# Order of the matmuls and of the activation steps in the up pass of a decoder layer

## The chip, the cores and the metric

One core of one Trainium2 chip runs one layer of a hybrid decoder. The metric is the device time of one execution in microseconds (us). The kernel before takes 1964.89 us, the median of three runs (1959.94 to 1966.12).

## What is computed

Two request groups (512 prompt tokens and 8 x 4 decode tokens, 544 in all) go through a mixer (attention and pooling) and then a feed-forward part; only the second one is touched here:

```python
def ffn_sublayer(x, w_up, w_down, g_pre, g_post):
    h = rmsnorm(x, g_pre)
    a = jnp.square(jax.nn.relu(jnp.einsum('ntd,df->ntf', h, w_up)))
    return x + rmsnorm(jnp.einsum('ntf,fd->ntd', a, w_down), g_post)
```

`w_up` is 2048 x 8192, `w_down` 8192 x 2048, all in float32.

## The kernel before

**Precision.** Every product is made of three matmuls in the rounded format fp32r: an operand is split into a high part (its rounded value) and a low part (what is left), and high x high, high x low and low x high are summed in one PSUM bank.

**The up pass.** The 8192 columns of `w_up` are taken in 32 blocks of 256. The first two are computed plainly; the other 30 (`UP_GROUPS`) are "groups" `G` of Strassen's method: seven products (`NP = 7`) of half-size matrices in place of eight. Product `N` is `G, i = divmod(N, NP)`, with `i` from 0 to 6. One product is 8 pairs of tiles, and so 24 matmuls of 128 x 128 weights by 272 columns. In `strassen_product` (line 2238) they are issued as 8 couples, high weight by high activation (L2263) and the same weight by low activation (L2264), then 8 with the low weight (L2268). Group G of the up pass is product 7G to 7G+6. The down pass follows, with products of 12 matmuls each.

**Who does what, for each product N.** ScalarE (ACT) rounds the weight twice: `high_copy` (L1169) into PSUM and `high_part` (L1178) into SBUF. VectorE (DVE) subtracts in `low_part` (L1669). GpSimd (POOL) makes four weight combinations in each group: t1 (L871), t3 (L876), t2 (L885), t4 (L891); i = 2 of a group needs t2, i = 3 t1, i = 4 t3 and i = 6 t4. DVE takes each product out of its bank and adds it into a quadrant sum: `take` (L1693, a copy, or L1696, an addition). A bank can only be written again after its `take`: by `taken_before` (line 2232) i = 2 of group G waits for the take of i = 0, and i = 5 for that of i = 3.

**The activation steps, once in a group.** When the takes of group G are done, DVE applies `relu` (L1703, after the take of the next group's i = 0), ACT squares (`square_mlp`, L1193), POOL forms four sums of quadrants (L899 to L904, `activation_sums`), ACT rounds seven rows (`mlp_high`, L1199), and DVE subtracts in two steps (`mlp_low`, L1715: three rows, then four). SyncE (SP) stores the result to HBM: high rows (L655), then the low rows (L660).

**What sets the order.** Each engine runs its instructions in program order; the loops are written out by hand. ACT's loop is `for N in range(4, N_ALL)` (line 1246), with `square_mlp(G + 1)` behind i = 3 and `mlp_high(G + 1)` behind i = 4. DVE's loop (line 1787) is, for each N: `take(N)`, `relu` where i = 0, `low_part(N + 3)`, and then `mlp_low(G + 1, 0)` where i = 3 and `mlp_low(G + 1, 1)` where i = 4. POOL's loop (line 911) is t4, activation sums, t1, t3, t2 of the next group. SP's queue, lines 689 to 694, is

```python
for g in range(1, UP_GROUPS - 1):
    store_hi(g + 1)
    store_lo(g + 1)
    if g < UP_GROUPS - 2:
        blocks_split(g)
        load_up(g + 2)
```

`store_lo` waits for each of the two steps of `mlp_low`; `load_up` fetches the 2 MB of weights of a group in four transfers (L626). t1 and i = 0 of a group wait for all four.

Of the kernel before, what the change touches and what calls it, by code (L numbers as in the profile page):

```python
# [24 lines left out]
def hybrid_decoder(nc, x_prompt, x_sample, cache_k, cache_v, state_pool, w_in, w_out, w_pool, pool_scale,  # L25
# [50 lines left out]
    UP_GROUPS = F_GROUPS - PLAIN  # L76
# [20 lines left out]
    with ExitStack() as ctx:  # L97
# [369 lines left out]
        STARTS = (True, True, False, True, False, False, False)  # L467
# [35 lines left out]
        def split_of(N, which):  # L503
            if N < N_UP:
                return splits[:, (N + 1) % 2 if N < NP else (N + 2) % 3, which, :].rearrange("p (j c) -> p j c", c=P)
            d = N - N_UP
            return splits[:, (2, 0)[d % 4 // 2], which, d % 2 * 512:(d % 2 + 1) * 512].rearrange("p (j c) -> p j c", c=P)
# [45 lines left out]
        for c, (bank, col) in enumerate(SPREAD_AT):  # L553
            first = c * P
            while first < c * P + tok_rows[c]:
# [4 lines left out]
                first = last  # L560
# [374 lines left out]
        def _(act):  # L935
# [160 lines left out]
            def square(src, count, par, tmp=sq_tmp):  # L1096


                group = 0 if not isinstance(count, int) else count // KT
                if isinstance(count, int) and count % KT < 2:  # L1100
                    if group:
                        act.wait_ge(sums_turned, group)
                else:
                    act.wait_ge(sq_added, count - 1 - group)
                nc.scalar.activation(tmp[:, par * T:(par + 1) * T].rearrange("p (h t) -> p h t", h=2), src,
                                     ACT.Square).then_inc(sq_ready, 1)
# [53 lines left out]
            def high_copy(N):  # L1160

                source_ready(N)
                if N < HIGH_FROM:
                    return
                if N < HIGH_FROM + 2:
                    act.wait_ge(relued, 4)
                if high_free(N):
                    act.wait_ge(part_lo, high_free(N))
                nc.scalar.activation(high_of(N).bitcast(F32R), weight_of(N), ACT.Copy).then_inc(hi_copied, 1)  # L1169

            def high_part(N):
                if N < 2:
                    act.wait_ge(unit_used, U_END - 1 + N)
                if N == NP + 2:
                    act.wait_ge(squared, PLAIN)
                if split_free(N):
                    act.wait_ge(product_done, split_free(N))
                nc.scalar.activation(split_of(N, 0), weight_of(N), ACT.Copy).then_inc(part_hi, 1)  # L1178
# [9 lines left out]
            def square_mlp(f):  # L1188
                act.wait_ge(relued, 4 * (f + 1) if f < PLAIN else 4 * PLAIN + 2 * (f - PLAIN + 1))
                if f == 1:  # L1190
                    act.wait_ge(lo_stored[0], 16)
                src = plain_rows if f == 1 else mlp_rows
                nc.scalar.activation(mlp_rows[:, 0:4, :], src[:, 0:4, :], ACT.Square).then_inc(squared, 1)  # L1193

            def mlp_high(g):
                act.wait_ge(a_summed, 4 * g + 4)
                if g > 0:
                    act.wait_ge(hi_stored, 16 * g)
                nc.scalar.activation(mlp_hi[:], mlp_sums[:], ACT.Copy).then_inc(mlp_rounded, 1)  # L1199
# [46 lines left out]
            for N in range(4, N_ALL):  # L1246
                high_copy(N)
                high_part(N)
                G, i = divmod(N, NP)
                if N == 5:  # L1250
                    mlp_high(1)
                if i == 3 and 0 < G < UP_GROUPS:
                    square_mlp(G + 1)
                if i == 4 and 0 < G < UP_GROUPS:
                    mlp_high(G + 1)
                if N == N_UP + NP + 3:
                    square_mlp(F_GROUPS - 1)
                if N == N_UP + 2 * NP + 2:
                    mlp_high(F_GROUPS - 1)
                n = G - (ALL_G - OUT_PAIRS)  # L1260
                if i == 5 and n > 0:
                    for nt in range(2):
                        m = 2 * (n - 1) + nt
                        act.wait_ge(taken, NP * G)
                        square(y_sum[:, m, :].rearrange("p (h t) -> p h t", h=2), 2 * KT + m, nt, sqf_tmp)
# [19 lines left out]
        def _(dve):  # L1285
# [385 lines left out]
            def take(N):  # L1671

                G, i = divmod(N, NP)
                dve.wait_ge(product_done, N + 1)
                src = banks[:, bank_of(G, i), 0:H]
                if G < UP_GROUPS:
                    at_quad = QUAD_AT[GOES_TO[i]]
                    dst, fresh = quads[:, at_quad + (G % 2 if at_quad == 3 else 0), :], FRESH[i]
                    if i == 0:
                        dve.wait_ge(h_summed, 4)  # L1680
                    if i == 0 and G > 1:
                        dve.wait_ge(relued, 4 * PLAIN + 2 * (G - 1))
                    if i == 2 and G > 0:
                        dve.wait_ge(relued, 4 * PLAIN + 2 * G)
                else:
                    c, n = divmod(G - UP_GROUPS, OUT_PAIRS)
                    dst, fresh = y_quad(n, GOES_TO[i]), FRESH[i] and c == 0
                    if c == 0 and n == 4 and i == 0:
                        dve.wait_ge(hi_stored, 16 * F_GROUPS)
                        for one in lo_stored:  # L1690
                            dve.wait_ge(one, 16 * F_GROUPS)
                if fresh:
                    nc.vector.tensor_copy(dst, src).then_inc(taken, 1)  # L1693
                else:
                    dve.wait_ge(taken, N)
                    nc.vector.tensor_tensor(dst, dst, src, ALU.add).then_inc(taken, 1)  # L1696
# [90 lines left out]
            for N in range(NP, N_UP):  # L1787
                take(N)
                G, i = divmod(N, NP)
                if i == 0:  # L1790
                    relu(G - 1)
                if N < N_UP - 3:
                    low_part(N + 3)
                elif N == N_UP - 3:
                    low_part(N_UP)
                    low_part(N_UP + 1)
                if i == 3:
                    mlp_low(G + 1, 0)
                if i == 4:
                    mlp_low(G + 1, 1)  # L1800
            low_part(N_UP + 2)
            low_part(N_UP + 3)
# [5 lines left out]
            for N in range(N_UP, N_ALL):  # L1808
# [8 lines left out]
                G, i = divmod(N, NP)  # L1817
# [32 lines left out]
        def _(pe):  # L1850
# [381 lines left out]
            def taken_before(G, i):  # L2232


                last_group = NP * (G - 1)
                return (last_group, last_group + 2, NP * G + 1, last_group + 6, NP * G + 3, NP * G + 4, NP * G + 5)[i]

            def strassen_product(N):
                G, i = divmod(N, NP)
                if N in (0, 1, 3, NP):  # L2240
                    pe.wait_ge(relued, {0: 5, 1: 6, 3: 7, NP: 8}[N])
                pe.wait_ge(part_hi, N + 1)
                if taken_before(G, i) > 0:
                    pe.wait_ge(taken, taken_before(G, i))
                if G == 0:
                    pe.wait_ge(hp_lo, H_READY[i])
                if G >= UP_GROUPS and (G - UP_GROUPS) % OUT_PAIRS == 0:
                    c = (G - UP_GROUPS) // OUT_PAIRS
                    pe.wait_ge(mlp_landed[i], 16 * (c + 1))
                out = banks[:, bank_of(G, i), 0:H]  # L2250
                pairs = UP_J if G < UP_GROUPS else DOWN_J

                def parts(j):
                    if G < UP_GROUPS:
                        return h_part(i, 0)[:, j, :], h_part(i, 1)[:, j, :]
                    c = (G - UP_GROUPS) // OUT_PAIRS
                    return mlp_parts[c % 2][i][:, j, 0, :], mlp_parts[c % 2][i][:, j, 1, :]

                for j in range(pairs):
                    xh, xl = parts(j)  # L2260
                    wh = split_of(N, 0)[:, j, :]
                    first = STARTS[i] and j == 0
                    nc.tensor.matmul(out, wh, xh, start=first, stop=False, skip_group_check=not STARTS[i])  # L2263
                    nc.tensor.matmul(out, wh, xl, start=False, stop=False, skip_group_check=not STARTS[i])  # L2264
                pe.wait_ge(part_lo, N + 1)
                for j in range(pairs):
                    xh, _ = parts(j)
                    ins = nc.tensor.matmul(out, split_of(N, 1)[:, j, :], xh, start=False, stop=j == pairs - 1,  # L2268
                                           skip_group_check=not STARTS[i])
                ins.then_inc(product_done, 1)  # L2270
# [69 lines left out]
```

## Time and profile before

| | |
|---|---|
| median of three runs | 1964.89 us |
| the profiled execution | 1960.73 us |
| its span, first to last instruction | 1959.0 us |
| TensorE (PE) busy | 1919.4 us, 98% |
| DVE, ACT, POOL busy | 67%, 64%, 44% |
| DMA engines, 1 queue of SP | 48.7% |
| granted TensorE clock, mean | 0.995 |

The profiled execution took 1.7 us more than its span; the rest of this text works with its span and its own time. Rows of the trace give an instruction's start in us from the start of the span, its duration, the engine, the line, what it writes and reads, and in square brackets how long the engine was idle before it and which instruction ended that. Consecutive instructions overlap by some 0.1 us: the next one starts before the last has drained. The up pass's groups run from 610 to 1254 us.

### The profile page before, as it was taken

Reading aid. Unit: us, or ns where it says so; the run is one execution under the profiler, and the core shown is the slowest. Engines: PE = TensorE matmul, PEld = TensorE weight load, DVE = VectorE, ACT = ScalarE, POOL = GpSimd, SP = SyncE. Lnnn points to the kernel's source line nnn. Section 1 sums busy time; section 2 is a strip of 40 time slices with the busy share of each in tenths; the row PEclk is TensorE's granted clock in tenths of the full one; section 3 lists DMA queues with packets and bytes.
Section 4 is the critical chain, followed back from the end, with each engine's and each line's share of the span. In section 5 each row is a group of like instructions: output and inputs, shape, how many; then the busy total and the mean of one; then the engine's idle time right before and its main releaser. Section 6 shows DMA issues by size and latency. Waiting matters only on the chain.

```text
span 1959.0 us, 38780 instructions
## 1 busy us (share of the span) xinstructions
PE 1919.4 (98%) x15210; PEld 1884.9 (96%) x15210; DVE 1318.6 (67%) x2014; ACT 1250.9 (64%) x1832; POOL 853.3 (44%) x625
## 2 busy tenths in 40 slices
PE   7999999999999999999999999999999999999998
PEld 7988899999889999999999999999999999999997
DVE  6566647222389777777777777776666666666687
ACT  6144424222376778777777777777777777777784
POOL 1000033111046566566566656545445545544572
PEclk9999999999999999999999999999999999999999
DMA  6422122522334555565565565975655655555542
GB/s 221 142 65 65 55 87 80 179 96 88 108 135 133 178 188 190 192 200 186 185 210 177 186 206 182 331 268 178 211 192 178 207 198 200 179 200 200 178 155 92
DMA packets 271756, 328.13 MB, mean 168 GB/s; under 512 B 8744, under 2 KB 237416, under 8 KB 270479
## 3 DMA queue, kind: packets, MB, share of 16 engines
q1 hardware_dynamic: 268208, 315.69, 48.7%
q10 hardware_dynamic: 3367, 9.96, 1.4%
q8 instruction: 122, 2.00, 0.4%
q14 instruction: 59, 0.48, 0.1%
HBM read 253.79 MB, written 74.22 MB: 167 GB/s over the span
## 4 chain that ended last, share of the span: by engine, by line
PE 92%; DVE 3%; DMA 2%; issue 1%; ACT 1%; POOL 1%; SPq 0%; DVEq 0%; ACTq 0%; POOLq 0%
PE banks L2263 22%; PE banks L1891 22%; PE banks L2264 21%; PE banks L2268 21%; PE banks L2219 1%; DMA mlp_kept<-mlp_rows 1%; PE banks L2196 1%; PE banks L2000 1%; PE banks L2031 1%; PE banks L2018 1%; PE banks L2285 0%; DVE w_lo L1296 0%; DMA w_raw<-in_w_in 0%; PE banks L1855 0%; DVE s_part L1720 0%
## 5 line engine op out<-in xcount | busy, mean ns | idle before, releaser
L2263 PE MATMUL banks<-mlp_part,splits 128*128 128x272 f32 x1792 | 467.3, 289 | 4.9 <-DVE y_sum L1693 4.3
L2264 PE MATMUL banks<-mlp_part,splits 128*128 128x272 f32 x1792 | 463.8, 286 | 0.0
L2263 PEld LDWEIGHTS banks<-mlp_part,splits 128*128 128x128 f32 x1792 | 336.0, 188 | 6.2 <-ACT splits L1178 3.0
L2264 PEld LDWEIGHTS banks<-mlp_part,splits 128*128 128x128 f32 x1792 | 336.5, 188 | 0.0
L1696 DVE TENSOR_TENSOR y_sum<-y_sum,banks 128x272 f32<-128x272 f32 x416 | 182.1, 438 | 179.7 <-PE banks L2268 179.6
L2268 PE MATMUL banks<-mlp_part,splits 128*128 128x272 f32 x1792 | 294.0, 286 | 0.0
L2263 PE MATMUL banks<-s_part,splits 128*128 128x272 f32 x960 | 249.7, 292 | 1.8 <-DVE quads L1693 1.8
L2268 PEld LDWEIGHTS banks<-mlp_part,splits 128*128 128x128 f32 x1792 | 250.2, 188 | 0.0
L2264 PE MATMUL banks<-s_part,splits 128*128 128x272 f32 x960 | 247.4, 289 | 0.0
L943 ACT ACTIVATE w_hi<-w_raw 128x1024 fp32r<-128x1024 f32 x74 | 78.2, 1058 | 262.4 <-PE banks L1891 259.5
L1891 PE MATMUL banks<-acts_hi,w_hi 128*128 128x288 f32 x1096 | 229.6, 291 | 12.2 <-DVE w_lo L1296 9.8
L1891 PE MATMUL banks<-acts_lo,w_hi 128*128 128x288 f32 x1096 | 226.8, 288 | 0.0
L1891 PE MATMUL banks<-acts_hi,w_lo 128*128 128x288 f32 x1096 | 225.8, 287 | 0.0
L1669 DVE TENSOR_TENSOR splits<-raw_up,banks 128x1024 fp32r<-128x1024 f32 x120 | 145.9, 1216 | 117.6 <-ACT banks L1169 117.6
L1178 ACT ACTIVATE splits<-raw_down 128x512 fp32r<-128x512 f32 x256 | 162.7, 636 | 92.8 <-PE banks L2268 92.7
L1296 DVE TENSOR_TENSOR w_lo<-w_raw,w_hi 128x1024 fp32r<-128x1024 f32 x74 | 100.0, 1353 | 174.4 <-ACT w_hi L943 174.2
L2263 PEld LDWEIGHTS banks<-s_part,splits 128*128 128x128 f32 x960 | 181.3, 189 | 6.0 <-ACT splits L1178 1.5
L2263 PE MATMUL banks<-base,splits 128*128 128x272 f32 x720 | 184.9, 289 | 0.6 <-DVE plain_rows L1709 0.6
L1891 PEld LDWEIGHTS banks<-acts_hi,w_hi 128*128 128x128 f32 x1096 | 167.9, 189 | 18.1 <-issue 15.7
L2264 PE MATMUL banks<-base,splits 128*128 128x272 f32 x720 | 184.7, 288 | 0.0
L2264 PEld LDWEIGHTS banks<-s_part,splits 128*128 128x128 f32 x960 | 181.9, 189 | 0.0
L1178 ACT ACTIVATE splits<-t_y 128x512 fp32r<-128x512 f32 (+1 forms) x188 | 144.3, 767 | 56.7 <-PE banks L2268 56.7
(273 smaller groups left out, 4299.9 us busy)
## 6 DMA issues: line engine op xcount, KB each, us to landing
raw_down<-in_w_down SPq DMA_DIRECT2D x128, 512.0 KB, 4.5
raw_up<-in_w_up SPq DMA_DIRECT2D x120, 512.0 KB, 6.7
mlp_part<-mlp_kept SPq DMA_DIRECT2D x56, 1088.0 KB, 8.4
mlp_kept<-mlp_hi SPq DMA_DIRECT2D x32, 952.0 KB, 4.5
w_raw<-in_w_in SPq DMA_DIRECT2D x40, 512.0 KB, 3.7
mlp_kept<-mlp_rows SPq DMA_DIRECT2D x32, 544.0 KB, 3.5
w_raw<-in_w_out SPq DMA_DIRECT2D x32, 512.0 KB, 3.4
mlp_kept<-mlp_rows SPq DMA_DIRECT2D x32, 408.0 KB, 2.6
```

The source lines that it names most:

```text
L943: nc.scalar.activation(w_hi[unit_place(k)][:], unit_raw(k), ACT.Copy).then_inc(hi_split, 1)
L1178: nc.scalar.activation(split_of(N, 0), weight_of(N), ACT.Copy).then_inc(part_hi, 1)
L1296: nc.vector.tensor_tensor(w_lo[unit_place(k)][:], unit_raw(k), w_hi[unit_place(k)][:].bitcast(F32), ALU.subtract).then_inc(lo_split, 1)
L1669: nc.vector.tensor_tensor(split_of(N, 1), weight_of(N), high, ALU.subtract).then_inc(part_lo, 1)
L1696: nc.vector.tensor_tensor(dst, dst, src, ALU.add).then_inc(taken, 1)
L1891: ins = nc.tensor.matmul(out, w, x[:, tokens], start=first, stop=last)
L2000: ins = nc.tensor.matmul(banks[:, 4 + h % 2, (h // 2) * 256 + lo:(h // 2) * 256 + 256], qT[rows, 2 * g + h // 2, blk * P:(blk + 1) * P], k ...
L2018: ins = nc.tensor.transpose(banks[:, 6, i * P:(i + 1) * P], probs[:, s % 2, 2 * r + hh, at:at + P], ident[:])
L2031: ins = nc.tensor.matmul(out, v_tok[:, blk - parts + 1 + half, g * HD:(g + 1) * HD], probs_T[:, :, i * P:(i + 1) * P], start=half == 0, st ...
L2263: nc.tensor.matmul(out, wh, xh, start=first, stop=False, skip_group_check=not STARTS[i])
L2264: nc.tensor.matmul(out, wh, xl, start=False, stop=False, skip_group_check=not STARTS[i])
L2268: ins = nc.tensor.matmul(out, split_of(N, 1)[:, j, :], xh, start=False, stop=j == pairs - 1, skip_group_check=not STARTS[i])
```

## The change

Three edits. In the up pass the 24 matmuls of a product are issued in three rounds (8 of high by high, 8 of high by low, 8 of low by high); the down pass keeps the couples. On ACT, `square_mlp` moves from behind i = 3 to behind i = 4 and `mlp_high` from i = 4 to i = 6. On DVE, the two steps of `mlp_low` move from i = 3 and 4 to i = 5 and 6. Nothing else differs: same instructions, same number.

```diff
@@ ScalarE, for N in range(4, N_ALL)
-                if i == 3 and 0 < G < UP_GROUPS:
+                if i == 4 and 0 < G < UP_GROUPS:
                     square_mlp(G + 1)
-                if i == 4 and 0 < G < UP_GROUPS:
+                if i == 6 and 0 < G < UP_GROUPS:
                     mlp_high(G + 1)
@@ VectorE, for N in range(NP, N_UP)
-                if i == 3:
+                if i == 5:
                     mlp_low(G + 1, 0)
-                if i == 4:
+                if i == 6:
                     mlp_low(G + 1, 1)
@@ TensorE, strassen_product
-                for j in range(pairs):
-                    xh, xl = parts(j)
-                    wh = split_of(N, 0)[:, j, :]
-                    first = STARTS[i] and j == 0
-                    nc.tensor.matmul(out, wh, xh, start=first, stop=False, skip_group_check=not STARTS[i])
-                    nc.tensor.matmul(out, wh, xl, start=False, stop=False, skip_group_check=not STARTS[i])
+                rounded = [(j, which) for j in range(pairs) for which in range(2)]
+                if G < UP_GROUPS:
+                    rounded.sort(key=lambda jw: jw[1])
+                for j, which in rounded:
+                    nc.tensor.matmul(out, split_of(N, 0)[:, j, :], parts(j)[which], start=STARTS[i] and j + which == 0,
+                                     stop=False, skip_group_check=not STARTS[i])
```

## Rows read from the trace of the kernel before

**Rows 1.** The page, busy time of each engine.
```profile
PE 1919.4 (98%) x15210; PEld 1884.9 (96%) x15210; DVE 1318.6 (67%) x2014; ACT 1250.9 (64%) x1832; POOL 853.3 (44%) x625
```
**Rows 2.** Busy time by stretch, in the middle of the up pass.
```profile
700.00:1220.00 520.00, 520.00 (x4110) 516.86 (x4109) 398.81 (x443) 399.53 (x391) 321.99 (x195) 1.00 0.60 193
```
**Rows 3.** Order of time on PE, products i = 3 to 5 of one group.
```profile
901.30 0.29 PE L2263 MATMUL banks<-s_part,splits 128*128 128x272 f32 x1
...
903.32 1.16 PE L2268 MATMUL banks<-s_part,splits 128*128 128x272 f32 x8
904.31 0.29 PE L2263 MATMUL banks<-s_part,splits 128*128 128x272 f32 x1
...
907.43 0.36 PE L2263 MATMUL banks<-s_part,splits 128*128 128x272 f32 x1
```
**Rows 4.** Order of time on DVE, the same group and into the next.
```profile
895.83 2.77 DVE L1703 SCALAR_TENSOR_TENSOR mlp_rows<-quads,ffn_scale 128x544 f32<-128x544 f32 x2
...
905.71 1.22 DVE L1669 TENSOR_TENSOR splits<-raw_up,banks 128x1024 fp32r<-128x1024 f32 x1 [3.44 <-ACT banks L1169]
906.85 0.43 DVE L1693 COPY quads<-banks 128x272 f32<-128x272 f32 x1
...
908.74 1.00 DVE L1715 TENSOR_TENSOR mlp_rows<-mlp_rows,mlp_hi 128x816 f32<-128x816 f32 x1
...
911.14 2.02 DVE L1715 TENSOR_TENSOR mlp_rows<-mlp_rows,mlp_hi 128x1088 f32<-128x1088 f32 x1
...
914.92 1.20 DVE L1669 TENSOR_TENSOR splits<-t_y,banks 128x1024 fp32r<-128x1024 f32 x1
...
917.11 2.76 DVE L1703 SCALAR_TENSOR_TENSOR mlp_rows<-quads,ffn_scale 128x544 f32<-128x544 f32 x2
```
**Rows 5.** Order of time on ACT, the same stretch.
```profile
898.64 1.12 ACT L1193 ACTIVATE mlp_rows<-mlp_rows 128x1088 f32<-128x1088 f32 x1 [2.10 <-DVE mlp_rows L1703]
...
902.97 1.80 ACT L1199 ACTIVATE mlp_hi<-mlp_rows 128x1904 fp32r<-128x1904 f32 x1 [1.32 <-POOL mlp_rows L904]
904.67 1.01 ACT L1169 ACTIVATE banks<-raw_up 128x1024 fp32r<-128x1024 f32 x1
...
912.25 1.01 ACT L1169 ACTIVATE banks<-t_y 128x1024 fp32r<-128x1024 f32 x1
```
**Rows 6.** Order of time on POOL, the same stretch.
```profile
902.89 2.41 POOL L871 TENSOR_TENSOR t_x<-raw_up 128x1024 f32<-128x1024 f32 x1
905.38 2.41 POOL L876 TENSOR_TENSOR raw_up<-raw_up 128x1024 f32<-128x1024 f32 x1
908.96 3.05 POOL L885 TENSOR_TENSOR t_y<-raw_up,t_x 128x1024 f32<-128x1024 f32 x1 [1.17 <-ACT splits L1178]
916.25 2.40 POOL L891 TENSOR_TENSOR t_y<-raw_up,t_y 128x1024 f32<-128x1024 f32 x1 [4.24 <-DVE splits L1669]
```
**Rows 7.** Order of time on SP's queue, the same stretch.
```profile
913.66 2.86 SPq L626 DMA_DIRECT2D raw_up<-in_w_up  x4
```
**Rows 8.** DMA issues, last of four loads at 916.0 and 937.3; us to landing.
```profile
raw_up<-in_w_up SPq DMA_DIRECT2D x1, 512.0 KB, 8.1
...
raw_up<-in_w_up SPq DMA_DIRECT2D x1, 512.0 KB, 7.6
```
**Rows 9.** Order of time on DVE, the second step of mlp_low in group 0.
```profile
615.11 1.28 DVE L1715 TENSOR_TENSOR mlp_rows<-mlp_rows,mlp_hi 128x1088 f32<-128x1088 f32 x1
```
**Rows 10.** Order of time on PE, products i = 3 and 4 of group 1.
```profile
644.53 1.27 PE L2268 MATMUL banks<-s_part,splits 128*128 128x272 f32 x8 [0.55 <-DVE splits L1669]
647.16 0.40 PE L2263 MATMUL banks<-s_part,splits 128*128 128x272 f32 x1 [1.36 <-DVE quads L1693]
```
**Rows 11.** Busy time by stretch; third from the end is the granted clock.
```profile
647.30:650.80 3.50, 3.50 (x17) 3.50 (x18) 0.37 (x1) 3.11 (x3) 3.42 (x3) 0.51 0.04 14
```
**Rows 12.** Order of time on DVE at the start of the down pass.
```profile
1255.60 0.43 DVE L1693 COPY y_sum<-banks 128x272 f32<-128x272 f32 x1
```
**Rows 13.** The page, weight loads of the second matmul of a couple.
```profile
L2264 PEld LDWEIGHTS banks<-s_part,splits 128*128 128x128 f32 x960 | 181.9, 189 | 0.0
```

## The prediction

> **What bounds the kernel now.** I read the page's busy times first: TensorE is busy 98% of the span [rows 1], and in the middle of the up pass all of it [rows 2]. That hides short gaps, because a matmul's row lasts 0.29 us while matmuls follow each other at about 0.126 us, so a gap under 0.16 us never shows as idle. Hence the order of time on PE. A product of 24 matmuls takes 904.31 - 901.30 = 3.01 us, of which the couples take 2.02 us (16 matmuls) and the last round 0.99 us (8): 0.126 and 0.124 us a matmul. From 904.31 to 907.43, however, it is 3.12 us, and the first matmul behind it is stretched by 0.07 us [rows 3]. So i = 5 starts some 0.18 us late. A group should last 7 x 3.013 = 21.09 us; the step from one relu to the same one in the next group, 917.11 - 895.83, says 21.28, and I use 21.27 [rows 4].
>
> Who makes i = 5 late is read on the other engines, backwards. It needs the take of i = 3 (906.85 to 907.28). That take stands behind the low part of i = 5, for which DVE idled 3.44 us waiting for ACT [rows 4]. ACT made that copy at 904.67, directly behind mlp_high, which waited 1.32 us for POOL's sums; these follow the square at 898.64, which waited 2.10 us for relu [rows 5]. This chain (relu, square, sums, mlp_high, copy, low part, take, PE) is what now sets the period, by 0.18 us over PE's own work.
>
> **The change, part by part.**
>
> *Three rounds.* No matmul is added. Every matmul has its weight load already, the second of a couple too (960 loads of 189 ns, overlapped) [rows 13], so a round with eight different weights costs what the low-weight round does: 0.124 to 0.126 us a matmul [rows 3]. In 30 x 7 products the difference of two readings of 0.01 us is at most 0.02 x 210 = 4 us either way; I take 0, since the two kinds of round agree within the reading.
>
> *Square later on ACT.* It no longer holds up the copies of i = 4; it starts when relu is done and both roundings of i = 4 are out, up to 0.9 us later than now. POOL's sums end near 903.7 in place of 902.9. t1 follows them, so this alone costs nothing that anyone waits for.
>
> *mlp_high later on ACT.* The copy of i = 5 is no longer behind it. The chain above is cut, and i = 5 starts on time: 0.18 us a group, some 5 us in 28 groups, if nothing else binds.
>
> *mlp_low later on DVE, and what hangs on it.* The second step now stands behind take(6) and behind low_part of the next group's i = 2. SP's queue waits for this step before it issues the low rows' store and, behind that, the four loads for the next group but one: the step ends at 913.16 and the loads start at 913.66 [rows 4, 7]. The last load is issued at 916.01 and lands 8.1 us later, at 924.1; one group on it is 937.33 + 7.6 = 944.9, with the step ending at 913.16 + 21.27 = 934.43. So the weights are there 10.9 and 10.5 us after the step [rows 8]; I take 10.7, and 10.4 to 11.0 as bounds. Today t1 of the next group starts at 902.89 + 21.27 = 924.2 [rows 6], right behind the landing: there is no slack in front of t1, only behind t2.
>
> Now the loop closes on itself, because low_part of i = 2 needs t2, and t2 needs t1, and t1 needs the landing. From the end M of the second step:
> - landing: M + 10.7
> - t1 starts 0.16 later and t3 2.49 after it, lasting 2.41 [rows 6]: landing + 5.06
> - the first step of mlp_low comes behind the low part of i = 1, whose copy also waits for the landing (two copies, one rounding and a low part on ACT and DVE: about 4.1 us), so it asks for its turn while t3 runs.
> - copy of i = 2 on ACT 0.03 + 1.01, low part 0.03 + 1.13, second step 1.28 [rows 4, 5, 9].
>
> What happens between the first step and t2 is a row's matter. t4 takes 2.40 us, but t2 took 3.05 when the first step (908.74 to 909.74) was running as it started; the second step took 2.02 us while t2 ran to 912.01 and 1.28 with POOL idle [rows 4, 6, 9]. POOL and this DVE instruction take turns: t2 ended 2.27 us after the step, and the step 1.15 us after t2. In the new place the first step waits for t3 and then takes about 0.87 us (its 1.00 less the same 0.13), and t2 ends 2.27 us behind it.
> The Trainium skill ("SBUF — State Buffer", "Who interferes with whom") has this as a rule: a VectorE instruction with two SBUF inputs and a GpSimd one that reads SBUF exclude each other, and the first to issue goes first. The trace agrees; by that rule the collision is certain (22.4 us below), and without it the sum is 21.7.
>
> Sum: 10.7 + 5.06 + 0.87 + 2.27 + 1.04 + 1.16 + 1.28 = **22.4 us** from M to the next M, once a group. That is longer than PE's 21.09. With the landing 10.4 or 11.0 us behind and 0.1 us of error in the rest it is 22.0 to 22.8.
>
> *How PE gets to wait.* Behind the second step on DVE stands take(0) of the new group, and i = 2 may not start before that take: PE starts i = 2 at M + 0.35 + 0.12. PE's own time for i = 2 would be 6.03 us into the group, so M may lie up to 5.4 us into it unpunished. Without any late load M would lie at 3.0 (take(6), low part, step). Following the loop, it moves to about 3.8, 4.5 and 5.8: four or five groups pass free, at 21.09 us; then each one lasts 22.4.
>
> *Sum over the pass.* Groups 7 to 29, 23 of them, 22.4 - 21.27 = 1.13 us more each: +26.0. Group 6 half in: +0.2. Groups 2 to 5: 4 x -0.18 = -0.7. Group 1: PE waited 0.55 and 1.36 us there [rows 10], the second wait for a take behind a low part that stands behind the square; with the square moved some 0.5 us of it goes, and 0.4 us of the later wait behind mlp_high. Then the clock had fallen to its lower level, 1.2 GHz, for 3.5 us [rows 11], which costs up to 1.7 us; it may or may not fall now. I take -2 (bounds -1 and -2.7). Down pass: the second step now comes behind the last take of the up pass, so the take of the first down product, at 1255.60 [rows 12], comes 1.2 us later and the third product some 0.4 us late: +0.4 (0 to 1.5). Together 26.0 + 0.2 - 0.7 - 2.0 + 0.4 = **+23.9 us**.
>
> The profiled execution took 1960.7 us, so 1984.6. The median of the runs is 4.2 us above it and the lowest run 0.8 below; I put the prediction a little above, at 1986.
>
> **Rivals.**
> - *The loads come in time* (ends on the other side). If the loop took under 21.1 us, that is, if the landing came 9.4 us behind the second step or the step were not behind low_part of i = 2, only the cut chain would count: 28 x -0.18 - 2 + 0.4 = -6.6, so 1954. Against it: the shorter of the two readings is 10.5 us, and the order is in the code. For it: an instruction order can free a resource that I haven't seen, such as ACT being early. 0.12.
> - *No collision of the first step with t2.* If DVE loses its turn to t2, or does its step sooner, 0.74 us drop out: 21.7 us a group, binding only after some 12 groups: 18 x 0.4 - 4 = +3, so 1964. The pair in rows 4 and 6 speaks against it. 0.08.
> - *The clock falls in every group.* PE now waits 1.3 us in one piece per group; in group 1, after 0.55 and 1.36 us of waits within 3 us, it fell for 3.5 us [rows 10, 11]. PE's group would be 21.09 + 1.7 = 22.8, over the loop's 22.4: 23 x 0.4 = +9 on top, 1995. It lies within the range of the main case and has 0.1 of its 0.80.
> - *The rounds cost* up to the 4 us of the bound above. With PE waiting 1.3 us a group anyway, they would vanish in that wait; no chance of its own.
>
> **How the numbers follow.** The loop case has 0.80. Its own range is from 22.0 us in 19 groups (19 x 0.73 - 2.2 = +12, 1972) to 22.8 us in 25 groups (25 x 1.53 - 1 + 1 = +38, 1999), and up to 2004 with the clock and the spread of the runs. For 8 in 10 over all cases the range must reach down to the collision case: 1964 to 2004. A measurement of this kernel can tell about 0.3%, 6 us, from no change. Slower by more: the loop case but its lowest tail, and a little of the second rival, 0.81. Within it: most of the second rival and that tail, 0.06. Faster: the first rival and a rest, 0.13.
>
> **What would show it.** In the trace after: the low part of i = 5 no longer waits for mlp_high; four or five groups at 21.09 us; then groups of 22.0 to 22.8 us, with one gap of about 1.3 us on PE before i = 2, released by the take of i = 0 (a copy, L1693); t1 released by the DMA in nearly every group in place of few; the first step of mlp_low near 1.7 us long and t2 near 3.1; the second step 1.3. Wrong would be: groups of 21.1 us to the end, or the loads landing under 10 us behind the step, or gaps that some other line releases.

## The result and the profile after

The changed kernel takes 1993.38 us (median; four runs, 1992.7 to 1996.72) against 1962.43 for the kernel before in its four runs: a ratio of 1.0161, 95% interval 1.0143 to 1.0178. It is 31 us slower. The profiled execution took 1994.05 us; its span is 1992.3 us, 33.3 more than before.

The page of the changed kernel, busy time and the chain that ended last:

```profile
span 1992.3 us, 38780 instructions
PE 1924.4 (97%) x15210; PEld 1887.9 (95%) x15210; DVE 1334.1 (67%) x2014; ACT 1251.7 (63%) x1832; POOL 879.0 (44%) x625
PE 67%; DMA 11%; POOL 9%; DVE 5%; SPq 3%; issue 3%; ACT 2%; POOLq 0%; DVEq 0%; ACTq 0%
```

The same chain of the kernel before:

```profile
PE 92%; DVE 3%; DMA 2%; issue 1%; ACT 1%; POOL 1%; SPq 0%; DVEq 0%; ACTq 0%; POOLq 0%
```

The number of instructions is the same. PE has 5 us more of busy time, but the chain tells more: DMA, POOL and SP's queue have taken a quarter of it from PE, so something other than matmuls set the time for a good part of the run. The busy times by stretch say where. The first row is the middle of the up pass, which before had no gap at all [rows 2]; the second is the first three groups of the down pass:

```profile
760.00:1281.00 521.00, 496.44 (x3904) 491.82 (x3903) 389.63 (x419) 381.80 (x377) 330.95 (x187) 1.00 0.57 185
1281.85:1324.60 42.75, 35.70 (x254) 34.42 (x253) 27.53 (x48) 24.75 (x42) 18.44 (x17) 0.92 1.01 339
```

The same three groups of the kernel before:

```profile
1253.85:1291.00 37.15, 32.30 (x254) 31.55 (x253) 26.34 (x47) 24.70 (x43) 18.50 (x17) 1.00 0.99 334
```

From the starts of the first matmul of each group, in order of time on PE, the 33.3 us divide so (us; the stretches that are not listed took 0.5 us less than before):

| | before | after | difference |
|---|---|---|---|
| up pass, group 1 | 25.49 | 22.49 | -3.0 |
| groups 2, 3, 4 | 63.83 | 63.27 (21.00, 21.00, 21.27) | -0.6 |
| groups 5 to 29 | 25 x 21.27 | 25 x 22.54 | +31.8 |
| down pass, first three groups | 37.2 | 42.8 | +5.6 |

Now one turn of the loop that was forecast, engine by engine. The changed kernel's PE at a gap, in order of time:

```profile
1129.98 1.16 PE L2268 MATMUL banks<-base,splits 128*128 128x272 f32 x8
1132.41 2.25 PE L2263 MATMUL banks<-s_part,splits 128*128 128x272 f32 x16 [1.27 <-ACT splits L1178]
```

Its DVE:

```profile
1108.05 1.28 DVE L1715 TENSOR_TENSOR mlp_rows<-mlp_rows,mlp_hi 128x1088 f32<-128x1088 f32 x1
...
1124.31 1.82 DVE L1715 TENSOR_TENSOR mlp_rows<-mlp_rows,mlp_hi 128x816 f32<-128x816 f32 x1
1126.06 0.43 DVE L1693 COPY quads<-banks 128x272 f32<-128x272 f32 x1
1129.49 1.22 DVE L1669 TENSOR_TENSOR splits<-t_y,banks 128x1024 fp32r<-128x1024 f32 x1 [3.00 <-ACT banks L1169]
1130.63 1.28 DVE L1715 TENSOR_TENSOR mlp_rows<-mlp_rows,mlp_hi 128x1088 f32<-128x1088 f32 x1
1131.83 0.43 DVE L1693 COPY quads<-banks 128x272 f32<-128x272 f32 x1
```

Its POOL, SP and ACT:

```profile
1120.35 2.42 POOL L871 TENSOR_TENSOR t_x<-raw_up 128x1024 f32<-128x1024 f32 x1 [3.22 <-DMA raw_up<-in_w_up]
1122.85 2.42 POOL L876 TENSOR_TENSOR raw_up<-raw_up 128x1024 f32<-128x1024 f32 x1
1125.21 3.18 POOL L885 TENSOR_TENSOR t_y<-raw_up,t_x 128x1024 f32<-128x1024 f32 x1
...
1109.84 2.85 SPq L626 DMA_DIRECT2D raw_up<-in_w_up  x4
...
1128.42 1.03 ACT L1169 ACTIVATE banks<-t_y 128x1024 fp32r<-128x1024 f32 x1 [4.30 <-POOL t_y L885]
1129.39 1.05 ACT L1178 ACTIVATE splits<-t_y 128x1024 fp32r<-128x1024 f32 x1
```

Read it from the second step's end at 1109.33. The loads are issued at 1109.84. The chain of waits has their landing at 1120.19, 10.86 us after the step. Then t1, t3, and t2, which ends at 1128.39 after 3.18 us, with the first step (1.82 us, not 1.00) in its way. The copy of i = 2, its low part, and the second step follow, to 1131.91: 22.58 us for the turn. The take behind it ends at 1132.26, and PE starts i = 2 at 1132.41. The profile names ACT as the releaser of PE, but ACT's instruction was over at 1130.44; i = 2 waits for both, and the take is the one that ended just before. The waits of all bound groups, from 696 to 1281 us, show that this turn is no exception (us in total, times, longest):

```profile
ACT banks L1169 <- POOL t_y L885: 108.8, 26, 4.3
POOL t_x L871 <- DMA raw_up<-in_w_up: 79.8, 25, 4.4
PE banks L2263 <- ACT splits L1178: 27.6, 23, 2.4
```

Before, POOL's t1 had waited for the DMA 0.6 us in all in the 520 us from 700 to 1220.

### The profile page after: what moved, and what is told of

It reads as the page before. It is cut to its first block, busy times and chain, and to the rows that moved or that the text cites. A ratio compares the mean times of both kernels' runs of the same rounds, so it can differ in the third digit from the quotient of the medians.

```text
span 1992.3 us, 38780 instructions
## 1 busy us (share of the span) xinstructions
PE 1924.4 (97%) x15210; PEld 1887.9 (95%) x15210; DVE 1334.1 (67%) x2014; ACT 1251.7 (63%) x1832; POOL 879.0 (44%) x625
## 4 chain that ended last, share of the span: by engine, by line
PE 67%; DMA 11%; POOL 9%; DVE 5%; SPq 3%; issue 3%; ACT 2%; POOLq 0%; DVEq 0%; ACTq 0%
PE banks L2263 26%; PE banks L1891 21%; PE banks L2268 13%; DMA raw_up<-in_w_up 9%; POOL t_y L885 4%; POOL t_x L871 3%; POOL raw_up L876 3%; SPq L626 3%; DVE mlp_rows L1715 2%; PE banks L2219 1%; ACT banks L1169 1%; PE banks L2196 1%; PE banks L2000 1%; PE banks L2031 1%; PE banks L2018 1%
## 5 line engine op out<-in xcount | busy, mean ns | idle before, releaser
L2263 PE MATMUL banks<-mlp_part,splits 128*128 128x272 f32 x3584 | 524.1, 288 | 7.0 <-DVE y_sum L1693 3.4
L2263 PEld LDWEIGHTS banks<-mlp_part,splits 128*128 128x128 f32 x3584 | 477.4, 188 | 8.9 <-issue 5.4
L2268 PE MATMUL banks<-mlp_part,splits 128*128 128x272 f32 x1792 | 294.9, 286 | 0.0
L2263 PE MATMUL banks<-s_part,splits 128*128 128x272 f32 x1920 | 265.5, 291 | 28.5 <-ACT splits L1178 27.6
L2263 PEld LDWEIGHTS banks<-s_part,splits 128*128 128x128 f32 x1920 | 248.9, 189 | 34.0 <-ACT splits L1178 31.9
L2268 PEld LDWEIGHTS banks<-mlp_part,splits 128*128 128x128 f32 x1792 | 251.2, 189 | 0.0
L1669 DVE TENSOR_TENSOR splits<-t_y,banks 128x512 fp32r<-128x512 f32 (+1 forms) x188 | 159.9, 851 | 76.4 <-ACT banks L1169 71.2
L1169 ACT ACTIVATE banks<-t_y 128x512 fp32r<-128x512 f32 (+1 forms) x188 | 135.7, 722 | 114.5 <-POOL t_y L885 114.3
L2263 PE MATMUL banks<-base,splits 128*128 128x272 f32 x1440 | 194.9, 287 | 0.6 <-DVE plain_rows L1709 0.6
L2263 PEld LDWEIGHTS banks<-base,splits 128*128 128x128 f32 x1440 | 185.7, 188 | 0.8 <-DVE plain_rows L1709 0.8
L1669 DVE TENSOR_TENSOR splits<-raw_down,banks 128x512 fp32r<-128x512 f32 x256 | 174.1, 680 | 1.5 <-ACT banks L1169 1.5
L1891 PEld LDWEIGHTS banks<-acts_hi,w_lo 128*128 128x128 f32 x1096 | 168.4, 189 | 0.0
```

The lines of the kernel that those rows point to most:

```text
L1669: nc.vector.tensor_tensor(split_of(N, 1), weight_of(N), high, ALU.subtract).then_inc(part_lo, 1)
L1891: ins = nc.tensor.matmul(out, w, x[:, tokens], start=first, stop=last)
L2263: nc.tensor.matmul(out, split_of(N, 0)[:, j, :], parts(j)[which], start=STARTS[i] and j + which == 0, stop=False, skip_group_check=not STA ...
```

## Experiments

Each ratio is to the kernel before on the same chip: 1960.27 us beside the rounds alone, the steps alone, the loads first and the steps behind i = 4 and 5; 1961.1 beside the others. "Late groups" are groups 5 to 29 of the up pass, on the mean, from the one trace that each kernel has.

**The rounds alone.** The kernel before with only the diff of `strassen_product`.

> The kernel before with the three rounds alone. My theory: the rounds don't carry the loss. A product takes 3.000 us in rounds (24 matmuls, read from the changed kernel) against 3.013 in couples, but the chain through relu, square and mlp_high sets the period and holds only three products, so 0.04 us a group: 1 to 3 us faster in all, groups of about 21.23 us. Rival: the rounds cost part of the loss by themselves, then 5 us or more slower than before.

1961.02 us, ratio 1.0003 (0.9993 to 1.0013). Late groups take 21.27 us, as before. The rounds carry none of the loss; nor do they give the 1 to 3 us that I expected. Something other than PE sets the period here (the chain), so this run could not show a cost or a gain of less than some 0.2 us a group.

**The steps alone.** The changed kernel with the couples back:

```diff
-                rounded = [(j, which) for j in range(pairs) for which in range(2)]
...
+                for j in range(pairs):
+                    xh, xl = parts(j)
...
```

> The changed kernel with the couples put back, so that only the activation steps are moved. My theory: the loop from the second step of mlp_low over the loads, t1, t3, t2 and low_part back to that step has no matmul in it, so the period of the late groups is again 22.5 us (22.3 to 22.8) and the time within 5 us of the changed kernel's 1993. Rival (the rounds carry some of it): below 1985.

1992.96 us, ratio 1.0169 (1.0155 to 1.0184); late groups 22.43 us. t1 waits for the landing as in the changed kernel:

```profile
POOL t_x L871 <- DMA raw_up<-in_w_up: 75.6, 25, 3.8
```

So the moved steps alone bring the whole loss. In groups 2 and 3, where no other engine holds PE up yet, the couples take 21.09 us; with rounds they take 21.00 in the changed kernel.

**The square alone.** The kernel before with one edit:

```diff
-                if i == 3 and 0 < G < UP_GROUPS:
+                if i == 4 and 0 < G < UP_GROUPS:
                     square_mlp(G + 1)
```

> The kernel before with only the square moved behind i = 4; mlp_high stays behind i = 4 too. My theory: the chain relu, square, sums, mlp_high, copy of i = 5, low part, take of i = 3, PE that sets the period of the kernel before gets longer by what the square now waits for on ACT (0.8 to 0.9 us), so groups of 22.0 to 22.2 us and 18 to 27 us slower than before: the move of the square pays only together with that of mlp_high. Rival (the chain isn't what sets the period before, but PE's own work with its waits): groups still near 21.3 us.

1984.65 us, ratio 1.0116 (1.0090 to 1.0142), late groups 22.07 us: 0.80 us a group more than before. ACT in order of time shows why; the square now comes behind a rounding that waits for PE:

```profile
906.76 1.06 ACT L1178 ACTIVATE splits<-raw_up 128x1024 fp32r<-128x1024 f32 x1 [1.04 <-PE banks L2268]
907.73 1.10 ACT L1193 ACTIVATE mlp_rows<-mlp_rows 128x1088 f32<-128x1088 f32 x1
```

This confirms the reading of the kernel before: a chain through relu, square, sums and mlp_high set its 21.27 us, not PE's own work.

**The second step ahead of the low part.** This leaves the step in the same turn of DVE's loop, but cuts the loop at the place where it waits for t2:

```diff
+                if i == 6:
+                    mlp_low(G + 1, 1)
                 if N < N_UP - 3:
                     low_part(N + 3)
...
-                if i == 6:
-                    mlp_low(G + 1, 1)
```

> The changed kernel with the second step of mlp_low put ahead of low_part in the same turn of DVE's loop (i = 6), so that it comes only 1.1 us of DVE's work sooner but doesn't wait for t2. My theory (a closed loop over t2): the step then ends about 2 us into the group whatever POOL does, the loads land 13 us into it, and groups take 21.0 to 21.2 us; 1955 to 1966. Rival (what costs is only how late in the group the step stands): the gain is about 1 us a group at most, so 21.4 us a group or more, 1968 to 1975.

1956.29 us, ratio 0.9965 (0.9950 to 0.9980). Every group from group 2 on takes 21.00 us. Swapping two neighbours on DVE takes away the loss and more; by the rival it would have been 21.4 us a group. t1 still waits for the landing, 1.2 us in each group, and t2 is out of the collision (2.41 us); it costs nothing, because nothing behind it comes back to the loads:

```profile
POOL t_x L871 <- DMA raw_up<-in_w_up: 29.3, 25, 1.7
```

**Less weight.** The last of the four loads brings one row of tiles in place of four, from the fourth group on. The products of the up pass are then made from partly stale weights.

```diff
+                n = 1 if g >= 3 and q == 3 else 4
-                sp.dma_start(raw_up[g % 2][:, 4 * q:4 * q + 4, :], w_up_v[q, :, :, ...
+                sp.dma_start(raw_up[g % 2][:, 4 * q:4 * q + n, :], w_up_v[q, :, 0:n, ...
```

> The changed kernel with the last of each group's four weight loads cut from four rows of tiles to one (384 KB of 2 MB less, from the fourth group on; the rest of the tile keeps older data, so that product is computed from partly stale weights). My theory: the landing comes 1.1 us sooner after the second step, and since the landing is in the loop, the period of the late groups falls by the same 1.1 us, from 22.5 to 21.4, the time to 1966 to 1976. Rival (the period is set by the engines' order and the DMA only looks late): no change of the period.

1955.06 us, ratio 0.9968 (0.9954 to 0.9983). Late groups take 21.00 us, not 21.4: the period did fall with the landing, but by more than I had said, and the time missed the expected range on the low side. POOL in order of time tells why (this kernel has one line more, so t1, t3, t2 are L872, L877, L886):

```profile
1106.06 2.42 POOL L872 TENSOR_TENSOR t_x<-raw_up 128x1024 f32<-128x1024 f32 x1 [0.50 <-DMA raw_up<-in_w_up]
1108.55 2.41 POOL L877 TENSOR_TENSOR raw_up<-raw_up 128x1024 f32<-128x1024 f32 x1
1110.92 2.41 POOL L886 TENSOR_TENSOR t_y<-raw_up,t_x 128x1024 f32<-128x1024 f32 x1
```

and DVE:

```profile
1113.77 1.00 DVE L1716 TENSOR_TENSOR mlp_rows<-mlp_rows,mlp_hi 128x816 f32<-128x816 f32 x1
```

t2 is over at 1113.33, before the first step begins, so the 0.78 us of the collision goes too. The last load landed 9.5 us behind the second step on the mean of the late groups, 1.3 sooner than in the changed kernel (10.9). 22.5 - 1.3 - 0.8 is 20.4 us, under PE's 21.0, and the loop no longer binds. In my expectation I had left the collision in.

**The first step out of POOL's way.** mlp_high behind i = 5, the first step ahead of the low part in the turn i = 3; the second step stays where the change put it.

```diff
-                if i == 6 and 0 < G < UP_GROUPS:
+                if i == 5 and 0 < G < UP_GROUPS:
                     mlp_high(G + 1)
...
+                if i == 3:
+                    mlp_low(G + 1, 0)
                 if N < N_UP - 3:
                     low_part(N + 3)
...
-                if i == 5:
-                    mlp_low(G + 1, 0)
```

> The changed kernel with the first step of mlp_low taken away from POOL's t3 and t2: mlp_high behind i = 5, the first step ahead of the low part in the turn i = 3, before the loads land. The second step stays behind the low part of the next group's i = 2. My theory: the loop stays closed, but t3 and t2 keep their 2.41 and 2.40 us, 0.78 us less than with the collision, so late groups take 21.7 to 21.9 us in place of 22.54, some 13 to 20 us below the changed kernel. Rival (the collision is beside the path): groups of 22.3 us or more.

1974.04 us, ratio 1.0066 (1.0049 to 1.0082), 19 us below the changed kernel. Late groups take 21.73 us, 0.81 less than 22.54. DVE and POOL in order of time:

```profile
1103.80 1.01 DVE L1715 TENSOR_TENSOR mlp_rows<-mlp_rows,mlp_hi 128x816 f32<-128x816 f32 x1 [1.77 <-ACT mlp_hi L1199]
```

```profile
1105.00 2.42 POOL L871 TENSOR_TENSOR t_x<-raw_up 128x1024 f32<-128x1024 f32 x1 [3.06 <-DMA raw_up<-in_w_up]
1107.49 2.42 POOL L876 TENSOR_TENSOR raw_up<-raw_up 128x1024 f32<-128x1024 f32 x1
1109.88 2.40 POOL L885 TENSOR_TENSOR t_y<-raw_up,t_x 128x1024 f32<-128x1024 f32 x1
```

The first step is over 0.2 us before t1 starts, t2 takes 2.40 us, and t1 still waits 3 us for the landing, so the loop is closed. On the mean of the late groups the last load lands 10.8 us behind the step, 0.1 sooner than in the changed kernel, and the rest of the turn is 0.7 us shorter: nearly all of the gain is the collision.

**The loads first.** SP's queue issues the loads ahead of the low rows' store.

```diff
                 store_hi(g + 1)
-                store_lo(g + 1)
                 if g < UP_GROUPS - 2:
                     blocks_split(g)
                     load_up(g + 2)
+                store_lo(g + 1)
```

> The changed kernel with the order of SP's queue changed: the loads of the next group but one are issued before the low rows' store, behind the high rows' store. DVE, ACT, POOL and PE keep the changed order. My theory: the loads' place behind the second step of mlp_low is what closes the loop; without it the weights land some 12 us sooner, POOL's t1 waits for no DMA, and groups take 21.0 to 21.1 us: 25 us or more below the changed kernel, at 1955 to 1968. Rival (DVE's order alone, with take(0) behind the late second step, costs the time): still 22 us a group.

1979.97 us, ratio 1.0088 (1.0073 to 1.0104): 13 us less than the changed kernel, where I had expected 25 or more. Late groups take 21.83 us, by turns near 21.1 and 22.4. The waits of the middle of the up pass:

```profile
POOL mlp_rows L899 <- ACT mlp_rows L1193: 119.8, 21, 6.3
DVE mlp_rows L1703 <- DMA mlp_kept<-mlp_rows: 111.5, 24, 5.3
```

SP's queue and relu in one group:

```profile
1111.42 3.08 SPq L660 DMA_DIRECT2D mlp_kept<-mlp_rows  x2
1120.00 1.36 DVE L1703 SCALAR_TENSOR_TENSOR mlp_rows<-quads,ffn_scale 128x544 f32<-128x544 f32 x2 [5.21 <-DMA mlp_kept<-mlp_rows]
```

The wait of t1 for the loads is gone from the waits, so that part held. In its place relu, which overwrites the rows that are stored, waits up to 5.3 us for the landing of the low rows' store: issued at 1111.42, behind 2 MB of weights, it lands at 1119.91. Everything behind relu slides, mlp_high too, and the high rows' store, which waits for mlp_high, stands ahead of the loads and of the next low rows' store in the queue. I read this as a second loop in the first one's place; no run cuts it, so that it sets the 21.83 us is argued and not shown.

**The last two groups early.** To see where the down pass loses 5.6 us:

```diff
+                late = G >= UP_GROUPS - 2
-                if i == 5:
+                if i == (4 if late else 5):
                     mlp_low(G + 1, 0)
-                if i == 6:
+                if i == (5 if late else 6):
                     mlp_low(G + 1, 1)
```

> The changed kernel with the steps of mlp_low behind i = 4 and 5 in the last two groups of the up pass only. My theory for the start of the down pass, whose first group takes 17.7 us against 11.3 before: SP's queue issues the first loads of the down pass only behind the low rows' store of the group before last, and this store moved into the last group. With the step early in the last two groups that stretch is back at 11 to 13 us, and the last groups save another 1 to 3 us: 5 to 9 us below the changed kernel. Rival (the down pass starts late for another reason, the clock or the takes): less than 2 us.

1992.43 us, ratio 1.0150 (1.0129 to 1.0172): 1 us below the changed kernel, where I had expected 5 to 9; by the time alone the rival would hold. The trace separates two things. The first three groups of the down pass take 38.9 us, 3.9 of the 5.6 back:

```profile
1280.04:1318.90 38.86, 33.90 (x254) 33.15 (x253) 26.34 (x47) 24.93 (x42) 18.55 (x17) 0.96 0.99 335
```

SP's queue fits that. In the changed kernel, then in this one, the first issues of the down pass:

```profile
1260.39 6.14 SPq L660 DMA_DIRECT2D mlp_kept<-mlp_rows  x2
1267.04 1.22 SPq L644 DMA_DIRECT2D raw_down<-in_w_down  x2
1268.31 4.09 SPq L663 DMA_DIRECT2D mlp_part<-mlp_kept  x4
```

```profile
1256.15 3.78 SPq L660 DMA_DIRECT2D mlp_kept<-mlp_rows  x2
1260.44 1.27 SPq L644 DMA_DIRECT2D raw_down<-in_w_down  x2
1261.76 4.69 SPq L663 DMA_DIRECT2D mlp_part<-mlp_kept  x4
```

The down pass's first matmuls come at 1281.85 and 1280.04, so its parts are asked for 13.5 and 18.3 us ahead. The DMA engines are busy throughout this stretch (share 1.01 and 0.99), and those 4.7 us are missed: the changed kernel's PE waited 2.8 us for a part, and behind that its granted clock fell (0.92 in the stretch; with the steps early it fell for a shorter time, 0.96):

```profile
1291.39 1.42 PE L2263 MATMUL banks<-mlp_part,splits 128*128 128x272 f32 x8 [2.81 <-DMA mlp_part<-mlp_kept]
```

But the last two groups took 22.3 and 22.7 us as before: the loads of the last one still stand behind a late step, and t1 waits 3.4 us for them. And in this execution the later groups of the down pass took 10.55 us in place of 10.45, which hid the rest (see the end). The other three executions of this kernel have no trace.

**Two versions that beat both kernels.** First, the changed kernel with the two steps of mlp_low behind i = 4 and 5.

```diff
-                if i == 5:
+                if i == 4:
                     mlp_low(G + 1, 0)
-                if i == 6:
+                if i == 5:
                     mlp_low(G + 1, 1)
```

> The changed kernel with the two steps of mlp_low behind i = 4 and 5 in place of 5 and 6; square and mlp_high stay late. My theory: the second step then stands ahead of the low part of i = 2 and no longer waits for t2, so the loop is open and the chain that set the period before is cut too: all groups from the third on take 21.0 us, PE has no wait in them, and the time is 8 to 14 us below the kernel before, 1950 to 1956. Rival (a late mlp_high alone delays stores and loads): groups over 21.3 us, not faster than before.

1953.80 us, ratio 0.9964 (0.9951 to 0.9976), late groups 21.14 us with no wait on PE, first three groups of the down pass 38.7 us. Then the same with mlp_high behind i = 5 and the steps behind 3 and 4:

> A version meant to beat both: the changed kernel (three rounds, square behind i = 4) with mlp_high behind i = 5 and the steps of mlp_low back behind i = 3 and 4. My theory: the chain before is cut and the loop is open, so groups take 21.0 to 21.15 us, and since the second step is as early as before, the start of the down pass takes its 37 us again (38.7 us with the steps behind 4 and 5): 1949 to 1954, 8 to 11 us below the kernel before and 0 to 2 below the variant with 4 and 5. Rival (mlp_high in front of the copy of i = 6 holds DVE up as it did at i = 5): groups over 21.2 us, no gain over the kernel before.

1951.66 us, ratio 0.9953 (0.9937 to 0.9969), late groups 21.14, the down pass's first three 37.2: some 9 us below the kernel before. The trace is of its slowest execution (1960.04; four of the six took 1950.4 to 1951.7). The intervals of these two and of the swap on DVE overlap; which is best isn't settled.

## Why the prediction was right

**What set the period before**: right. Cutting the chain gave groups of 21.00 to 21.14 us wherever the loop was open, and lengthening it by the square's wait gave 22.07.

**The loop**: right in mechanism, place and size. Its turn was forecast at 22.4 us and measured 22.54 as the mean of the late groups, 22.42 in groups 10 to 29, 22.58 in the turn shown; landing 10.86 us after the step (10.7 forecast), first step 1.82 and t2 3.18 us (1.7 and 3.1 forecast), take to PE 0.15. Three runs hold it up from different sides: cutting it at the low part (21.00), taking the collision out of it (21.73), shortening the landing (21.00). The 0.78 us of t2 come and go with the first step's place (3.18 us in the changed kernel, 2.40 to 2.41 in all three). This agrees with the rule that the prediction took from the Trainium skill ("SBUF — State Buffer", "Who interferes with whom").

**When it starts to bind**: too late, and worked out wrongly. I had four free groups (2 to 5) and half of group 6; the trace has two at 21.00, a third at 21.27, and then the 25 late ones in place of 23. The second step's end lay 3.0 us into group 2, as forecast, but then at 4.5, 5.6 and 6.8 where I had 3.8, 4.5 and 5.8. The prediction's own terms don't give its figures: a turn of 22.4 us against groups of 21.09 moves the step by 1.31 us a group, to 4.3, 5.6 and 6.9, and the room for it, 6.03 - 0.35 - 0.12, is 5.6 us and not 5.4. With them the loop binds from group 5 on, as it did. Groups 5 to 9 took 8.7 us more than before, where the sum had 3.4; groups 10 to 29 took 23.0 more, and the sum had 22.6 for them.

**The clock** fell twice in the late groups, in groups 6 and 9 (24.68 and 25.22 us); one of the two gaps on PE, and the stretch around it, with a granted clock of 0.76:

```profile
816.77 3.10 PE L2263 MATMUL banks<-s_part,splits 128*128 128x272 f32 x16 [2.43 <-ACT splits L1178]
815.00:822.00 7.00, 5.23 (x29) 5.26 (x30) 7.00 (x8) 5.79 (x7) 4.35 (x3) 0.76 0.67 211
```

Sixteen matmuls take 3.10 us there in place of 2.25. The two gaps, 1.88 and 2.43 us, are the longest of the up pass, and each comes behind one of the two latest landings of the loop (11.6 and 12.0 us behind the step); behind the other gaps, of up to 1.74 us, the clock stayed. The rival with the clock was in the range; it came twice and not in each group. Groups 5 to 9 together took 3.0 us more than five turns of 22.42. In group 1 the clock did not fall this time, and the group gave back 3.0 us where I had 2.

**The start of the down pass** was the step that was mis-sized: forecast +0.4 us, from DVE's take alone, measured +5.6. I had followed the second step on SP's queue to the loads of the up pass, but not to the first issues of the down pass, which stand behind the same store. The run with the last two groups early gives back 3.9 of it. The remaining 1.7 were not taken apart by a run of their own, but the two versions that beat both kernels point at the same place: 38.7 us with the steps behind i = 4 and 5, 37.2, as before, with the steps behind 3 and 4.

**The three rounds**: right at 0, with an interval of 1 part in 1000 either way where the chain sets the period. Where PE does, the groups took 21.09 us with couples and 21.00 or 21.14 with rounds (see the end): less than 0.1 us a group either way.

The sum was +23.9 us, the span grew by 33.3: 5.7 more from the loop's start and size, 5.2 more from the down pass, 1.0 less in group 1, and 0.5 less in the stretches that are not in the table. The two large errors lie on the same side, so it was not errors that cancel that put the result into the range.

## What to carry to other kernels

When an instruction is moved on an engine that issues in order, follow what waits for it on the DMA queue as far as the transfers behind it, and from their landing back to the place where the instruction now stands. If that way closes and is longer than the busiest engine's own work, its length is the new period, however idle each engine in it looks. Of two neighbours on an engine, put the one that a transfer waits for ahead of the one that waits for another engine: here that swap was worth 37 us. And when a queue is reordered instead, ask what then stands behind the large transfer.

## What the runs showed of the hardware that was not expected

The spacing of matmuls takes two values, a little under 1% apart, for the same instructions. In the down pass a group of 84 matmuls takes 10.453 us in some traces (before, the changed kernel, the rounds alone) and 10.547 in others (loads first, less weight, the last two groups early), each constant to 0.002 us except in the first three and the last five groups. In the last round of each product, the kernel before and then the run with the last two groups early, 1.49 and 1.51 us from one product to the next:

```profile
1502.59 0.66 PE L2268 MATMUL banks<-mlp_part,splits 128*128 128x272 f32 x4
1504.08 0.66 PE L2268 MATMUL banks<-mlp_part,splits 128*128 128x272 f32 x4
1505.57 0.66 PE L2268 MATMUL banks<-mlp_part,splits 128*128 128x272 f32 x4
```

```profile
1502.21 0.67 PE L2269 MATMUL banks<-mlp_part,splits 128*128 128x272 f32 x4
1503.72 0.67 PE L2269 MATMUL banks<-mlp_part,splits 128*128 128x272 f32 x4
1505.23 0.67 PE L2269 MATMUL banks<-mlp_part,splits 128*128 128x272 f32 x4
```

The granted clock is 1.00 in both. In the up pass the rounds show 21.00 us a group in some traces and 21.14 in others, with no wait on PE in either, and the two passes don't go together: with less weight it is 21.00 and 10.547, with the steps behind i = 4 and 5 it is 21.14 and 10.453. Over the 61 later groups of the down pass it makes 5.7 us; the kernel before spreads over nearly 10 us in its own runs (1957.5 to 1967.2 us). What decides it wasn't tried, and with one trace for each kernel the record can't say whether it goes with the kernel or with the execution. It is why 5 us in one pair of traces must not be read as the effect of an edit before the spacing in a stretch without waits has been compared.
